# Sparse attention in a two-block transformer kernel: the mask moved into the gates, fewer and wider ScalarE instructions, and output products between the last pairs

## What is computed

```
for each of 16 heads (4 groups of keys and values), each token t:
    p_c = masked_softmax(q . k_cmp + bias)    # 15 compressed blocks, block j visible if t >= 16 j + 31
    p_s = masked_softmax(q . k_sel + bias)    # causal, 256 keys
    p_w = masked_softmax(q . k_win + bias)    # causal, 256 keys
    o   = g_c * p_c v_cmp + g_s * p_s v_sel + g_w * p_w v_win
masked_softmax(s, mask) = where(mask, softmax(where(mask, s, -1e30)), 0)
h = layer_norm(alpha * h + concat(o) @ w_o)
```

## Time and profile before

| | |
|---|---|
| three runs | 2323.48, 2324.93, 2326.65 us; median 2324.93 |
| the profiled execution | 2319.89 us |
| its span in the trace | 2317.7 us |
| TensorE busy | 2231.2 us, 96% |
| VectorE busy | 1607.3 us, 69% |
| ScalarE busy | 1178.3 us, 51% |

### The profile page before, as it was taken

One profiled execution on the slowest core, in us unless ns is written; L12 is line 12 of the kernel. 1 busy time (PEld: TensorE's weight loads), 2 busy tenths in 40 slices (PEclk: granted clock), 3 DMA queues, 4 the chain that ended last, 5 costly groups with the idle time before them and its releaser, 6 DMA issues. The chain is left out here.

```text
span 2317.7 us, 36494 instructions
## 1 busy us (share of the span) xinstructions
PE 2231.2 (96%) x14340; PEld 1993.7 (86%) x14340; DVE 1607.3 (69%) x2801; ACT 1178.3 (51%) x2054; POOL 57.3 (2%) x28
## 2 busy tenths in 40 slices
PE   8878999999999999999999999999999999989998
PEld 8877788899999998888888889988888788868887
DVE  7866557999888986666657566766657555686555
ACT  6522445455554445556555455545443544575444
POOL 0131000010000000000000000000000000000000
PEclk9999999999999999999999999999999999999999
DMA  7472324455444445655555556536555655404552
GB/s 269 146 73 97 127 108 167 139 179 186 146 151 146 145 150 182 194 195 191 194 174 213 194 186 235 195 129 235 181 190 190 240 183 191 156 2 164 200 188 102
DMA packets 78306, 390.18 MB, mean 168 GB/s; under 512 B 9771, under 2 KB 12715, under 8 KB 49740
## 3 DMA queue, kind: packets, MB, share of 16 engines
q1 hardware_dynamic: 76684, 383.59, 47.3%
q0 software_dynamic: 1040, 4.19, 1.7%
q10 hardware_dynamic: 432, 0.33, 0.0%
HBM read 382.83 MB, written 5.24 MB: 167 GB/s over the span
## 5 line engine op out<-in xcount | busy, mean ns | idle before, releaser
L252 DVE TENSOR_TENSOR split_slots<-ring,split_slots 128x1024 fp32r<-128x1024 f32 x402 | 479.9, 1238 | 134.5 <-ACT split_slots L243 134.4
L243 ACT ACTIVATE split_slots<-ring 128x1024 fp32r<-128x1024 f32 x402 | 402.2, 1054 | 154.7 <-PE banks L396 138.4
L2977 PE MATMUL banks<-x_transposed,split_slots 128*128 128x512 f32 x1360 | 478.6, 395 | 2.0 <-PEq L460 2.0
L405 DVE SCALAR_TENSOR_TENSOR expert_lo<-ring,expert_hi 128x512 fp32r<-128x512 f32 x512 | 362.4, 713 | 170.2 <-ACT expert_hi L400 169.1
L400 ACT ACTIVATE expert_hi<-ring 128x512 fp32r<-128x512 f32 x512 | 323.9, 634 | 263.8 <-PE banks L396 263.8
L2978 PE MATMUL banks<-x_transposed,split_slots 128*128 128x256 f32 x1360 | 381.6, 281 | 0.0
L2977 PEld LDWEIGHTS banks<-x_transposed,split_slots 128*128 128x128 f32 x1360 | 255.3, 188 | 62.3 <-issue 2.2
L394 PE MATMUL banks<-x_transposed,expert_hi 128*128 128x256 f32 x1024 | 295.2, 288 | 6.6 <-DVE expert_lo L405 6.6
L395 PE MATMUL banks<-x_transposed,expert_hi 128*128 128x256 f32 x1024 | 288.9, 282 | 0.0
L396 PE MATMUL banks<-x_transposed,expert_lo 128*128 128x256 f32 x1024 | 288.8, 282 | 0.0
L2978 PEld LDWEIGHTS banks<-x_transposed,split_slots 128*128 128x128 f32 x1360 | 256.4, 189 | 1.5
(11 more groups left out here) (490 smaller groups left out, 4148.2 us busy)
## 6 DMA issues: line engine op xcount, KB each, us to landing
ring<-in_ffn_w SPq DMA_DIRECT2D x132, 1024.0 KB, 4.8
ring<-in_peer_u SPq DMA_DIRECT2D x128, 512.0 KB, 3.4
ring<-in_peer_v SPq DMA_DIRECT2D x128, 512.0 KB, 3.5
ring<-in_w_in SPq DMA_DIRECT2D x16, 1024.0 KB, 5.1
ring<-in_sgu_w_in SPq DMA_DIRECT2D x16, 1024.0 KB, 4.8
ring<-in_peer_wq SPq DMA_DIRECT2D x8, 1024.0 KB, 6.3
ring<-in_sgu_w_out SPq DMA_DIRECT2D x8, 1024.0 KB, 4.8
ring<-in_kv_w SPq DMA_DIRECT2D x6, 1024.0 KB, 4.9
```

The lines of the kernel that those rows point to most:

```text
L243: act.activation(self.parts[:, b, 0, p], self.k.w.slot(g)[:, p], ACT.Copy).then_inc(self.high_done, 1)
L252: ins = dve.tensor_tensor(self.parts[:, b, 1, p], self.k.w.slot(g)[:, p], self.parts[:, b, 0, p].bitcast(F32), ALU.subtract)
L405: return dve.scalar_tensor_tensor(dst, src, scale, hi.bitcast(F32), ALU.mult, ALU.subtract)
L2977: pe.matmul(out(j, slice(0, 2 * SEQ)), lh, k.xT.both[:, c, :, :], start=(c == 0), stop=False)
```

## The change

- The mask goes. Instead `mask_gates` multiplies, once, the compressed gate of the tokens of the first tile with whether they see any block. `guard` goes with it.
- VectorE adds the negated maximum to the 60 compressed scores (`shift`), and ScalarE takes one exponential over all 60 columns instead of four over 15 with a bias each.
- The three tiles of a head's turned probabilities become one tile of 1024 columns (the name `probabilities_T` stays), and `copy` is one activation over both banks, of all 128 partitions.
- ScalarE's order in a step becomes: copy of the first head, exponentials over 256 columns, copy of the second head, exponentials over 128, the compressed one, output. VectorE's steps between its maxima move by one place.
- The stand-ins go. The products of w_o's first slot, 24 of 96, are made inside the loop: 12 at the start of step 8, 12 in step 9 after the last turn. The split of w_o's first slot (`rows.high(0)`, `rows.low(0)`) moves from step 8 to steps 0 and 2, and the second slot is split in step 8.

The diff, without the changed counts of semaphores (5 per pair become 3, 3 copies become 1) and other lines that only follow:

```diff
-def out_and_norm(k, aT, slots, gains, which):
+def out_and_norm(k, aT, slots, gains, which, ahead=None):
...
-        split = Splitter(k, ctx, g0)
+        split = ahead or Splitter(k, ctx, k.w.take(slots))
+        split_ahead, used_ahead = (2, 1) if ahead else (0, 0)
+        split.before = k.before
...
-            for m in range(slots - 2):
+            for m in range(used_ahead, slots - 2):
...
-            for m in range(slots):
+            for m in range(split_ahead, slots):
...
+        rows = Splitter(k, ctx, k.w.take(4))
+        rows.before = None
...
-        pT = [k.sb(ctx, f"probabilities_T_{b}", [P, 2, 2, A]) for b in range(turned_sets)]
-        pT_last = [k.sb(ctx, f"probabilities_last_T_{b}", [P, 2, A]) for b in range(turned_sets)]
-        cT = [k.sb(ctx, f"cmp_probabilities_T_{b}", [16, SEQ]) for b in range(turned_sets)]
+        turned_T = [k.sb(ctx, f"probabilities_T_{b}", [P, 8, A]) for b in range(turned_sets)]
+        pT, pT_last, cT = ([t[:, n:m, :] for t in turned_T] for n, m in ((0, 4), (4, 6), (6, 8)))
...
-            k.stream(sp)
+            k.w.issue(sp, rows.g0 + RING)
...
+        def output_product(pe, i):
+            if i == 0:
+                pe.wait_ge(biased, 3 * NH // 2)
+                pe.wait_ge(written, 2)
+                rows.ready(pe, 0)
+            wh, wl = rows.rows(0)
+            for r in range(2):
+                ins = down_tile(pe, k, k.xT.at(slice(0, P), r), (wh[:, r, :], wl[:, r, :]), i, r == 0, False)
+            if i == 1:
+                ins.then_inc(rows.eaten, 1)
...
                 if n == NH // 2:
-                    pe.wait_ge(biased, 3 * NH // 2)
-                    stand_in(pe, k, 6)
-                if n == NH // 2 + 1:
-                    stand_in(pe, k, 4)
-                    pe.wait_ge(expd, NH // 2)
-                    stand_in(pe, k, 12)
+                    output_product(pe, 0)
                 if 2 <= n < NH // 2 + 2:
                     turn(pe, 2 * (n - 2))
-                if n >= NH // 2 + 1:
-                    stand_in(pe, k, 5)
-                if n >= 3:
+                if 3 <= n < NH // 2 + 2:
                     mix(pe, n - 3)
                 if 2 <= n < NH // 2 + 2:
                     turn(pe, 2 * (n - 2) + 1)
+                if n == NH // 2 + 1:
+                    output_product(pe, 1)
+                if n == NH // 2 + 2:
+                    mix(pe, n - 3)
                 if n == 2:
                     queries(pe, 3, (0,))
...
-        def mask(dve, q):
+        def mask_gates(dve):
...
+            own = gates[:, :, :].rearrange("p i (h n) -> p i h n", n=3)[:, 0, :, 0]
+            dve.wait_ge(narrow_read, 2)
+            dve.tensor_tensor(own, own, masks[:, 0, 0:1].broadcast_to([P, NH]), ALU.mult).then_inc(gates_masked, 1)
+        def shift(dve, q):
             own = cs[q % 3][:, :, :, 0:NCMP]
-            dve.wait_ge(expd, q + 1)
-            dve.tensor_tensor(own, own, masks[:, :, 0:NCMP].unsqueeze(1).broadcast_to([P, 2, TILES, NCMP]), ALU.mult).then_inc(vs, 1)
+            dve.wait_ge(negmax, 3 * q + 3)
+            dve.tensor_tensor(own, own, spread(c[q % 3][:, 0, :, :, 0], NCMP), ALU.add).then_inc(shifted, 1)
...
-        def guard(dve, q):
-            dve.wait_ge(vs, 5 * q + 2)
-            dve.tensor_scalar(flat(q, 1), flat(q, 1), 1e-30, None, ALU.max).then_inc(vs, 1)
...
-            steps = [mask, total, guard, inverse, gate, weigh] if last is not None else []
+            steps = [total, inverse, gate, weigh] if last is not None else []
...
             ins.then_inc(biased, 1)
-            between()
             dve.wait_ge(biased, 3 * q + 1)
             dve.tensor_reduce(c[b][:, 0, :, 1, 1:3], second[b][:, :, :, :], AX_X, ALU.max, negate=True).then_inc(negmax, 1)
             between()
             between()
             dve.wait_ge(biased, 3 * q + 3)
             dve.tensor_reduce(c[b][:, 0, :, :, 0], cs[b][:, :, :, 0:NCMP], AX_X, ALU.max, negate=True).then_inc(negmax, 1)
-            for _ in range(3):
-                between()
+            between()
...
+            shift(dve, q)
+            between()
...
-                        dve.wait_ge(narrow_read, 2)
+                        mask_gates(dve)
                     pair(dve, n, n - 1)
                     if n == 1:
                         queries_out(2)
+                    if n == 2:
+                        rows.low(dve, 0)
...
-                    for step in (mask, total, guard, inverse, gate, weigh):
+                    for step in (total, inverse, gate, weigh):
                         step(dve, n - 1)
-                    begin.lows(dve)
                 if n >= 4:
                     output(n - 4)
+            rows.low(dve, 1)
...
-            def exps(q):
-                b = q % 3
-                for i, scored_of, done in ((1, second, 1), (0, first, 2)):
-                    act.wait_ge(negmax, 3 * q + done)
-                    for hh in range(2):
-                        for branch in range(2):
-                            act.activation(scored_of[b][:, hh, branch, :], scored_of[b][:, hh, branch, :], ACT.Exp,
-                                           bias=c[b][:, 0, hh, i, branch + 1:branch + 2],
-                                           accum_out=c[b][:, 1, hh, i, branch + 1:branch + 2])
-                act.wait_ge(negmax, 3 * q + 3)
+            def exps(q, i):
+                b, scored_of = q % 3, (first, second)[i]
+                act.wait_ge(negmax, 3 * q + 2 - i)
                 for hh in range(2):
-                    for i in range(TILES):
-                        ins = act.activation(cs[b][:, hh, i, 0:NCMP], cs[b][:, hh, i, 0:NCMP], ACT.Exp,
-                                             bias=c[b][:, 0, hh, i, 0:1])
-                ins.then_inc(expd, 1)
+                    for branch in range(2):
+                        act.activation(scored_of[b][:, hh, branch, :], scored_of[b][:, hh, branch, :], ACT.Exp,
+                                       bias=c[b][:, 0, hh, i, branch + 1:branch + 2],
+                                       accum_out=c[b][:, 1, hh, i, branch + 1:branch + 2])
+            def cmp_exps(q):
+                own = cs[q % 3][:, :, :, 0:NCMP]
+                act.wait_ge(shifted, q + 1)
+                act.activation(own, own, ACT.Exp).then_inc(expd, 1)
...
-                flat = lambda ap: ap.rearrange("p a n -> p (a n)")
-                act.activation(pT[b][:, :, :, :].rearrange("p a i n -> p (a i n)"), k.psum[:, 4, :], ACT.Copy).then_inc(copied, 1)
-                act.activation(flat(pT_last[b][:, :, :]), k.psum[:, 5, 0:B], ACT.Copy).then_inc(copied, 1)
-                act.activation(cT[b][0:NCMP, :], k.psum[0:NCMP, 5, B:2 * B], ACT.Copy).then_inc(copied, 1)
+                act.activation(turned_T[b][:, :, :].rearrange("p a n -> p (a n)"),
+                               k.psum[:, 4:6, :].rearrange("p b n -> p (b n)"), ACT.Copy).then_inc(copied, 1)
...
                     copy(2 * (n - 2))
+                if n < NH // 2:
+                    exps(n, 1)
+                if 2 <= n < NH // 2 + 2:
                     copy(2 * (n - 2) + 1)
                 if n < NH // 2:
-                    exps(n)
+                    exps(n, 0)
+                    cmp_exps(n)
...
+                    split.finished(act, 1)
+                    rows.high(act, 0)
                 if n == 3:
                     queries_out(3)
                 if n == NH // 2:
-                    begin.highs(act)
+                    rows.high(act, 1)
...
-        k.before = Before((written, NH // 2), (high, NH // 2), (written, NH // 2), ((copied, 3 * NH),),
-                          parts=lambda m, i: 2 * m + 2)
+        k.before = Before((split.eaten, QUERIES), (high, NH // 2), (written, NH // 2), parts=lambda m, i: 2 * m + 2)
+        return rows
```

More of the change, by code:

```diff
@@ L3581, in query_and_attend @@
         turned_sets = 4
-        pT = [k.sb(ctx, f"probabilities_T_{b}", [P, 2, 2, A]) for b in range(turned_sets)]
-        pT_last = [k.sb(ctx, f"probabilities_last_T_{b}", [P, 2, A]) for b in range(turned_sets)]
-        cT = [k.sb(ctx, f"cmp_probabilities_T_{b}", [16, SEQ]) for b in range(turned_sets)]
+        turned_T = [k.sb(ctx, f"probabilities_T_{b}", [P, 8, A]) for b in range(turned_sets)]
+        pT, pT_last, cT = ([t[:, n:m, :] for t in turned_T] for n, m in ((0, 4), (4, 6), (6, 8)))
         c = [k.sb(ctx, f"softmax_columns_{b}", [P, 3, 2, TILES, 3]) for b in range(3)]
-        landed, scored, biased, negmax, expd, vs, weighed, turned, copied, outs, high, written = \
-            (k.sig.new() for _ in range(12))
-        begin = Beginning(k)
+        landed, scored, biased, negmax, shifted, expd, vs, weighed, turned, copied, outs, high, written = \
+            (k.sig.new() for _ in range(13))
+        gates_masked = k.sig.new()
         def parts(h):
```

23 lines of the change are left out of this document (12 added, 11 removed).

## The result

The changed kernel takes **2309.27 us**, the median of four runs (2305.35 to 2311.69), the kernel before 2324.91 beside it: a ratio of 0.9939, 95% interval 0.9926 to 0.9951. It is faster by 15.6 us, with 13.8 forecast; 2311.1 was the forecast time, 2307 to 2317 the range.

A forecast was written before the change was run, and what follows sets the result against it. The prediction took ScalarE's period with its round trip to TensorE as the bound, VectorE next; 3.8 (loop) + 4.4 (its end) + 5.6 (output stage) = 13.8 us off the 2324.93 median gave 2311.1 us, range 2307 to 2317.

The forecast's parts named there:

- What bounds the kernel: Attention's pair loop: ScalarE sets the 7.93 us period, with a 1.25 us wait for TensorE's transposes; afterwards VectorE, 6.53 us.
- The loop, 3.8 us: Pair loop up to pair 7's start: 2068.4 instead of 2072.21, so 3.8 us gained.
- The loop's end, 4.4 us: From pair 7's start to the last mix's end: 20.9 us instead of 25.3, so 4.4 us gained.
- One sign that the prediction named as speaking against it: Loop's end: the forecast is wrong if TensorE's record shows head 12's turns waiting behind the first products.
- The output stage, 5.6 us: After the last mix: 24 of 96 products already done, at 0.234 us each, 5.6 us gained.
- The clock: Loop and output stage: removing the stand-ins leaves the granted clock at 1.00, so nothing is charged.
- the rival: From the first product on, TensorE falls to 1.2 GHz: 22.5 us lost against 13.8 gained, 2333.6 us; chance 0.03.
- The loop keeps its period: Pair loop: longer handover chain keeps the period at 7.9 us, 3.8 us not gained, 2314.9 us; chance 0.12.
- The products stay on the path: Loop's end: the output products are merely moved, 3.4 us less gain, 2314.5 us; chance 0.1.
- A transfer or split is late: Output stage: slot 3's load and split come late, at most 2 + 5 us, 2318.1 us; chance 0.04.

## Why the prediction was right, and where it was not

**What bounds the kernel** was right. ScalarE's period with one round trip to TensorE was read from a wait of 1.25 us; put back, the wait had that length again, and taken out of the kernel before by the order alone, it left VectorE's 6.81 as the period to 0.01 us.

**The loop, 3.8 us.** Measured 3.88. The places where it was said to be gained or lost all show: pair 2 unmoved, pair 3 0.32 later for the slot's low part (0.4 forecast), pair 5 0.47 earlier (0.56), then periods of 6.47 (6.53). VectorE's sum was 0.06 too large, since the maximum, shift and weighing run in 0.46 us, not 0.53. The wide exponential holds ScalarE 0.14 us, not 0.25, and the copy 0.90, not 0.95. The 0.14 lies below the prediction's lower bound of 0.20, the price of one small exponential: that one had a bias, and without it the small ones take 0.42 / 4 = 0.105. Neither size mattered, because ScalarE has room; it would have, had ScalarE stayed the bound. (The prediction also speaks of eight exponentials of 256 columns; there are four, with four accumulator reads, and their 1.97 us was read rightly.)

**The loop's end, 4.4 us.** Measured 25.27 - 20.80 = 4.47. Its size was right, and so were its times: from pair 7's start the turn of head 12 ends after 7.6 us (7.7 forecast), mix 5 after 9.6 (9.7), copy 14 after 14.8 (14.8), the turn of head 15 after 15.8 (16.0), the products after 18.8 (18.8). **Its reason was wrong in one clause**: "the removed stand-ins being most of what ran there". They filled time in which TensorE would have waited. Taken out of the kernel before, they cost 3.54 us instead of giving any back, and in the new order they cost 0.52 against fills that fit. In their place the runs show four steps. From pair 7's start to the end of the last mix it takes 25.27 us before, 23.10 with the new order, 22.57 with transposes in place of the stand-ins, 18.94 in the changed kernel with its products after the last mix, and 20.80 with the products in the loop.

The third step, 3.63 us, is the largest, and the prediction has no term for it. The traces show where most of it lies: from the start of head 14's turn to the start of mix 6 it takes 3.68 us with transposes (2089.80 to 2093.48) and 1.00 in the other kernel (2085.10 to 2086.10), 2.68 less. VectorE's timeline of the kernel with transposes gives the reason:

```profile
2090.64 2.36 DVE L303 TENSOR_TENSOR split_slots<-ring,split_slots 128x1024 fp32r<-128x1024 f32 x2 [1.43 <-ACT split_slots L297]
2092.92 0.75 DVE L405 SCALAR_TENSOR_TENSOR x_transposed<-banks,x_transposed 128x256 fp32r<-128x256 f32 x2
```

Mix 6 waits for the first of the two outputs at 2092.92 (output 4), which stands behind a slot's low part in VectorE's list. The changed kernel has a slot's low part in its end too, slot 1's; but its list has output 4 ahead of it, and mix 6 does not wait:

```profile
2084.16 0.42 DVE L405 SCALAR_TENSOR_TENSOR x_transposed<-banks,x_transposed 128x256 fp32r<-128x256 f32 x1
2086.41 2.36 DVE L252 TENSOR_TENSOR split_slots<-ring,split_slots 128x1024 fp32r<-128x1024 f32 x2 [1.83 <-ACT split_slots L243]
```

So this change of place, an output ahead of a split, is worth more than half of the 4.47 us, which the prediction put down mostly to the stand-ins. It is read from the traces; no run moved it alone. Of the other 0.95 us some 0.43 are the wide forms, by the run that undid them, and the rest (mask and guard among it) was not taken apart.

**One step of the end was a tie, not a delay.** The prediction put slot 1's high part ahead of copy 14 and let the turn of head 15 wait for it. Copy 14 ends at 2088.51, mix 6 at about 2088.6; the turn starts at 2088.66 without a recorded wait. TensorE's own chain (turn 14, mix 6, turn 15) is as long. One sign that the prediction named as speaking against it did show: the turn of head 12 waits behind the first products. It is 0.28 us, and the sum had charged 0.4 for it.

**The output stage, 5.6 us.** Measured 22.50 - 16.90 = 5.60. Of the 24 products made earlier 3.74 us are hidden (3.4 forecast).

**The clock** was charged nothing, which was right for the changed kernel. The ground given, that pauses get shorter and real products take the stand-ins' place, is borne out as far as the runs go: empty pauses in the old kernel cost 3.54 us (2.24 in the new order), filled ones cost no clock. But the chance of 0.03 leaned on the loop's 1.00 as if the stand-ins had no part in it. They had, in the kernel before: without them the clock fell twice behind pair 7. So the rival was nearer than it looked, though with the products after the last mix the clock stayed at 1.00 too. Its price for one fall, 1.7 us, was close to the 1.8 that each slow mix cost. Its reading that the clock was back within 3.5 us of products at 2005 is a little short: in that trace it is at 1.00 from 2008.75 on.

**The rivals.** "The loop keeps its period" fell with the 6.47. "The products stay on the path" fell with the 3.74. "A transfer or split is late" fell with the 16.90.

**The forecast time** took 5.04 us between profiled execution and median as given. After, the profiled execution lay 2.42 above its median, so the forecast missed by 1.8 us while the stretch missed by 0.15: what remains is the scatter of the rest of the kernel. That the time came out so close is in part luck: in another group of runs the kernel before had a median of 2322.09 us, and from there the gain would be 12.8.

## What to carry to other kernels

Where an engine makes two reads of the same buffer with a round trip to another engine between them, put its independent work between the reads, not after them: that alone took 5.28 us off the kernel before, where the whole change takes 13.95, and shortened the end of the loop as well as its period. After such a step the next engine's work per period was the new period here; widened instructions on an engine that now has room gave 0.51. In an engine's fixed list, put what another engine waits for ahead of what nobody wants yet: output 4 ahead of a split, 2.68 us by the traces. A stand-in in a wait cost nothing here while it fitted the wait; replace it with real work rather than delete it, and look at the granted clock of the stretch when you do.

## What was not expected of the hardware

- The clock fell to 1.2 GHz in the loop's end when TensorE's pauses of 1.51 and 2.26 us, and later 2.61, were left empty (0.51 in the window from 2084 to 2090), and the stretch grew by 3.54 us. In another kernel with an empty pause of 2.35 us it stayed at 1.00. What decides between them stays open.
- With 16 transposes in each pause the clock was 1.00 as with products, in one execution each; the loop has 2.04 of TensorE's 5.93 us of work per pair in transposes and held 1.00.
- An exponential of 60 columns without a bias holds ScalarE 0.14 us from start to start (0.24 its own time), less than one of 15 columns with a bias, 0.20. Four of 15 columns take 0.79 us with a bias and 0.42 without, so dropping the bias saves 0.37 us per pair and the one wide instruction 0.28 more. The shift that replaces the bias costs VectorE 0.13, and VectorE is the busier engine; no run took the shift out, so what the trade as a whole is worth stays open.
